# Four of the modulation sums moved from TensorE's matmuls to VectorE's multiply-adds

## The reference

```
c_act = jax.nn.silu(c)
mod = c_act @ mod_w[i] + mod_b[i]
sh_m, sc_m, gt_m, sh_f, sc_f, gt_f = [m[:, None, :] for m in jnp.split(mod, 6, axis=-1)]
h = rmsnorm(x, norm_pre_mix[i]) * (1.0 + sc_m) + sh_m
y = conformer_conv_module(h, ...)       # h @ w1, gate, depthwise convolution of width 31, layernorm, @ w2
x = x + gt_m * rmsnorm(y, norm_post_mix[i])
h = rmsnorm(x, norm_pre_ffn[i]) * (1.0 + sc_f) + sh_f
y = conv_ffn(h, ...)
```

## Time and profile before

| What | Value |
|---|---|
| Median of 3 runs | 1467.34 us (1464.78 to 1468.24) |
| The profiled execution | 1466.46 us |
| Its span in the trace | 1464.7 us |
| Granted clock over the span | 0.996 |
| TensorE / VectorE / ScalarE / GpSimd busy | 97% / 65% / 47% / 11% |
| The stretch of the convolution steps | about 55 to 129 us |

### The profile page before, as it was taken

One profiled execution on the slowest core, in us unless ns is written; L12 is line 12 of the kernel. 1 busy time (PEld: TensorE's weight loads), 2 busy tenths in 40 slices (PEclk: granted clock), 3 DMA queues, 4 the chain that ended last, 5 costly groups with the idle time before them and its releaser, 6 DMA issues.

```text
span 1464.7 us, 31335 instructions
## 1 busy us (share of the span) xinstructions
PE 1419.9 (97%) x12736; PEld 1293.8 (88%) x12737; DVE 951.1 (65%) x1289; ACT 683.9 (47%) x879; POOL 155.5 (11%) x178
## 2 busy tenths in 40 slices
PE   6999999999999999999999999999999999999997
PEld 4767789999999998988889999999999898899996
DVE  3657676667655556695677556575566678855656
ACT  4445654545534336744435343353434466534332
POOL 1343032231000004012300000000000012000000
PEclk9999999999999999999999999999999999999999
DMA  9984466666666655421026666666666344576662
GB/s 345 329 314 183 148 201 187 194 178 179 182 192 182 185 157 166 144 87 57 9 87 200 183 191 186 187 187 187 186 186 195 121 145 148 164 216 191 186 186 86
DMA packets 293909, 257.75 MB, mean 176 GB/s; under 512 B 7104, under 2 KB 270272, under 8 KB 290752
## 3 DMA queue, kind: packets, MB, share of 16 engines
q1 hardware_dynamic: 293824, 256.49, 57.3%
HBM read 255.42 MB, written 1.05 MB: 175 GB/s over the span
## 4 chain that ended last, share of the span: by engine, by line
PE 50%; DVE 4%; ACT 1%; issue 0%; DVEq 0%; ACTq 0%
PE ps L145 14%; PE ps L146 14%; PE ps L147 14%; PE ps L2306 3%; PE ps L383 1%; DVE stats L342 1%; DVE arena L340 1%; PE ps L390 1%; PE ps L469 0%; PE ps L474 0%; PE ps L470 0%; PE ps L2289 0%; PE ps L2297 0%; DVE gate_m L2609 0%; PE ps L2792 0%
## 5 line engine op out<-in xcount | busy, mean ns | idle before, releaser
L145 PE MATMUL ps<-actT,a_parts 128*128 128x256 f32 x2096 | 589.1, 281 | 8.0 <-DVE a_parts L130 4.2
L146 PE MATMUL ps<-actT,a_parts 128*128 128x256 f32 x2096 | 585.8, 279 | 0.0
L147 PE MATMUL ps<-actT,a_parts 128*128 128x256 f32 x2096 | 585.4, 279 | 0.0
L145 PEld LDWEIGHTS ps<-actT,a_parts 128*128 128x128 f32 x2096 | 394.8, 188 | 17.7 <-DVE a_parts L130 6.7
L146 PEld LDWEIGHTS ps<-actT,a_parts 128*128 128x128 f32 x2096 | 394.6, 188 | 4.2
L147 PEld LDWEIGHTS ps<-actT,a_parts 128*128 128x128 f32 x2096 | 394.6, 188 | 0.0
L1329 DVE TENSOR_TENSOR a_parts<-a_raw,a_parts 128x2048 fp32r<-128x2048 f32 x100 | 239.1, 2391 | 55.8 <-ACT a_parts L1326 55.6
L1343 DVE TENSOR_TENSOR b_parts<-b_raw,b_parts 128x1024 fp32r<-128x1024 f32 x72 | 88.2, 1225 | 160.3 <-ACT b_parts L1340 160.3
L1326 ACT ACTIVATE a_parts<-a_raw 128x2048 fp32r<-128x2048 f32 x100 | 190.3, 1903 | 0.7 <-DMA a_raw<-in_ffn_w_up 0.7
L1340 ACT ACTIVATE b_parts<-b_raw 128x1024 fp32r<-128x1024 f32 x90 | 95.2, 1058 | 171.0 <-PE ps L147 171.0
L145 PE MATMUL ps<-b_parts,hid 128*128 128x512 f32 x400 | 158.1, 395 | 1.2 <-DVE hid L1440 1.2
(11 more groups left out here) (387 smaller groups left out, 1820.1 us busy)
## 6 DMA issues: line engine op xcount, KB each, us to landing
a_raw<-in_ffn_w_gate SPq DMA_DIRECT2D x88, 512.0 KB, 4.0
a_raw<-in_ffn_w_up SPq DMA_DIRECT2D x88, 512.0 KB, 5.2
b_raw<-in_ffn_w_down SPq DMA_DIRECT2D x88, 512.0 KB, 3.3
arena<-in_mod_w SPq DMA_DIRECT2D x24, 1024.0 KB, 9.5
a_raw<-in_f_up_w SPq DMA_DIRECT2D x44, 512.0 KB, 5.0
b_raw<-in_f_down_w SPq DMA_DIRECT2D x22, 512.0 KB, 3.3
a_raw<-in_rwkv_w_in SPq DMA_DIRECT2D x10, 1024.0 KB, 5.4
a_raw<-in_sb_w_in SPq DMA_DIRECT2D x10, 1024.0 KB, 5.2
```

The source lines that it names most:

```text
L145: pe.matmul(out, lhs[0], rhs[0], start=start, stop=False)
L146: pe.matmul(out, lhs[0], rhs[1], start=False, stop=False)
L147: return pe.matmul(out, lhs[1], rhs[0], start=False, stop=stop)
```

## The change

In steps j = 0 to 3 the second chunk of the unit (9, 11, 13 and 15) is no longer summed by TensorE. VectorE does it with 8 instructions of 128 x 256: it multiplies depth part 0 by silu(c), one value per partition, and then adds part after part, each step waiting for the one before. What is left has a part of the sum on all 128 partitions, so `mod_post` uses a weight `ones` (128 x 128, all 1) for these chunks instead of `sel`. ScalarE's copy of the four chunks goes as well. Buffers of these chunks are free again by a new semaphore `mod_added`, and GpSimd sets `ones` once at the start.

```diff
+            ON_DVE = [9, 11, 13, 15]
             def load_mod(sp, i):
                 if i >= MOD_SLOTS:
-                    sp.wait_ge(mod_used, i - MOD_SLOTS + 1)
+                    if i - MOD_SLOTS in ON_DVE:
+                        sp.wait_ge(mod_added, on_dve(i - MOD_SLOTS))
+                    else:
+                        sp.wait_ge(mod_used, on_pe(i - MOD_SLOTS))
...
+            def mod_add(dve, i):
+
+                dve.wait_ge(mod_loaded[i % MOD_SLOTS], 16 * (i // MOD_SLOTS + 1))
+                dve.wait_ge(mod_posted, (i - 2) // 2 + 1 if i < 18 else i - 9)
+                total = modp[:, i % 2]
+                for k in range(KD):
+                    rows_k = mods[:, i % MOD_SLOTS, k * MOD_COLS:(k + 1) * MOD_COLS]
+                    if k == 0:
+                        ins = dve.tensor_scalar(total, rows_k, csilu[:, 0:1], None, ALU.mult)
+                    else:
+                        ins = dve.scalar_tensor_tensor(total, rows_k, csilu[:, k:k + 1], total, ALU.mult, ALU.add)
+                    if k < KD - 1:
+                        dve_steps.step(dve, ins)
+                ins.then_inc(mod_added, 1)
...
             def mod_post(pe, u):
 
-                pe.wait_ge(mod_taken, unit_chunks(u)[-1] + 1)
+                last = unit_chunks(u)[-1]
+                pe.wait_ge(mod_taken, on_pe(last))
+                if last in ON_DVE:
+                    pe.wait_ge(mod_added, on_dve(last))
...
-                                            modp[:, i % 2, h * P:(h + 1) * P], sel[:, 0:1], start=True, stop=True)
+                                            modp[:, i % 2, h * P:(h + 1) * P],
+                                            (ones if i in ON_DVE else sel)[:, 0:1], start=True, stop=True)
...
+                    pool_steps.step(pool, pool.memset(ones, 1.0))
...
                         for i in unit_chunks(UNIT_AT[j]):
-                            mod_take(act, i)
+                            if i not in ON_DVE:
+                                mod_take(act, i)
...
                         for i in unit_chunks(UNIT_AT[j]):
-                            mod_sum(pe, i)
+                            if i not in ON_DVE:
+                                mod_sum(pe, i)
...
                     for j in range(KD):
+                        if j < 4:
+                            mod_add(dve, unit_chunks(UNIT_AT[j])[-1])
                         for g in SPLIT_AT.get(j, ()):
                             ring_a.split_lo(dve, g)
```

More of the change, by code:

```diff
@@ L552, in first_block @@
         def first_block():
-            mods, u_pad, taps_w, shifted, conv, sq, sig, rstd, modp, stat32, sel, mask32, ones_mean = carve(
+            mods, u_pad, taps_w, shifted, conv, sq, sig, rstd, modp, stat32, sel, mask32, ones_mean, ones = carve(
                 (MOD_SLOTS, ACH), (2, PAD + SEQ + 2), (2, QUAD * TAPS), (2 * 4, SHIFT_LEN), (KD, SEQ), (KD, SEQ),
-                (2, SEQ), (SEQ,), (2, MOD_COLS), (KD, QUAD), (P,), (QUAD,), (P,))
+                (2, SEQ), (SEQ,), (2, MOD_COLS), (KD, QUAD), (P,), (QUAD,), (P,), (P,))
             hT = sq
@@ L576, in first_block @@
                                                                          "post_read"))
+            mod_added = sem("mod_added")
             cond_ready, cond_sig = sem("cond_ready"), sem("cond_sig")
@@ L598, in mod_bank, with on_dve, on_pe @@
                 return 2 + i % 2 if i < 8 else (3, 7)[i % 2] if i < 16 else 3 if i < 20 else 4 + i % 2
+            ON_DVE = [9, 11, 13, 15]
+            def on_dve(i):
+                return sum(1 for v in ON_DVE if v <= i)
+            def on_pe(i):
+                return i + 1 - on_dve(i)
             def post_bank(u):
@@ L611, in mod_sum @@
                 if i >= 2:
-                    pe.wait_ge(mod_taken, i if 17 <= i < 20 else i - 1)
+                    pe.wait_ge(mod_taken, on_pe(i - 1) - (i < 9))
                 if 8 <= i < 16 and i % 2:
@@ L620, in mod_take @@
             def mod_take(act, i):
-                act.wait_ge(mod_used, i + 1)
+                act.wait_ge(mod_used, on_pe(i))
                 if i >= 2:
@@ L625, in mod_take @@
                 act.activation(modp[:, i % 2], ps[:, mod_bank(i), 0:MOD_COLS], ACT.Copy).then_inc(mod_taken, 1)
+            def mod_add(dve, i):
[11 more added lines that the diff above has]
+                ins.then_inc(mod_added, 1)
             def mod_copy(dve, i):
-                dve.wait_ge(mod_used, i + 1)
+                dve.wait_ge(mod_used, on_pe(i))
                 dve.wait_ge(mod_posted, i - 9)
@@ L646, in mod_post @@
                             ps[:, 6 + c // 2, (c % 2) * MOD_COLS:(c % 2 + 1) * MOD_COLS]
-                        ins = pe.matmul(out_, sel, modp[:, i % 2], start=True, stop=True)
+                        ins = pe.matmul(out_, ones if i in ON_DVE else sel, modp[:, i % 2], start=True, stop=True)
                 ins.then_inc(mod_posted, 1)
```

## The result

The changed kernel took 1479.43 us (median of 6, 1478.42 to 1480.49) against 1466.66 us for the kernel before on the same chip (median of 6): 12.8 us more, ratio 1.0084 with a 95% interval of 1.0073 to 1.0094. The time forecast was 1476.6, the range 1469.5 to 1479.5. The median lies 0.07 us inside the upper end, and three of the six runs (1479.73, 1480.12 and 1480.49) lie above it. The profiled execution is one of these, 1480.12 us; its trace spans 1478.2 us, 13.5 more than before.

What follows compares the result with a forecast made beforehand. TensorE, busy 97% of the span, was taken to bound the kernel. 4.8 - 0.875 - 0.875 + 3.6 = +6.7 us, with the clock's +3.4 +10.1, on 1466.46 gave 1476.6 us; range 1469.5 to 1479.5.

Steps and rivals of the forecast that it cites:

- longer steps on VectorE: Rival: VectorE's sum steps take more than 0.52 us each, giving 1477.6 or 1479.4 us; chance 0.10.
- What bounds the kernel: TensorE, busy 97% of the span: whatever it wins or loses in steps 0 to 3 arrives at the end.
- The length of a sum: One chunk's sum on VectorE: seven steps of 0.52 us and a first of 0.39, 4.0 us, between 3.4 and 4.5.
- The blocking by GpSimd: GpSimd's taps halt VectorE's sum in steps 0 and 3, 1.8 us each; rival without blocking, chance 0.14.
- Steps 0 to 3: TensorE 4.8 us late in step 0, 0.875 gained in each of steps 1 and 2, 3.6 late in step 3.
- The stalls: TensorE stands waiting for VectorE's sum, about 5.7 us in step 0 and 5.1 us in step 3.
- The margin of step 1: VectorE's sum of chunk 11 is done at 75.2, 1.3 us before TensorE's convolution ends at 76.5.
- The transfers: Chunk 13's issue waits until 65.4 for VectorE's sum of chunk 9; the delay is covered and costs nothing.
- The clock: TensorE's clock halves after each of two stalls, 3.4 us in all; rival of one fall or none, with blocking, 0.27.
- the stretch at 741: Around 741 us TensorE stood 1.3 us and its clock fell from 2.4 to 1.2 GHz, priced at 1.7 us.

Runs made afterwards that it cites:

- e3_taps: e1_wait with GpSimd's taps of steps 2 and 5 held back until VectorE's sums of chunks 9 and 15 are done; 1474.46 us, +7.4 against before.
- e4_mid: e1_wait with only chunks 11 and 13 on VectorE, 9 and 15 staying on TensorE; 1471.51 us, +4.4 against before.
- e11_busy13: e8_busy with 13 unused matmuls instead of 10 filling TensorE's stall in step 3; 1473.05 us, +6.8 against before.
- e1_wait: Changed kernel with TensorE's wait before the sums of chunks 20 to 23 set back to the copy of the same bank's last chunk; 1478.16 us, +11.1 against before.
- e5_first: e1_wait with only chunk 9 on VectorE, 11, 13 and 15 staying on TensorE; 1471.64 us, +4.6 against before.
- e2_busy: e1_wait with unused matmuls on constants filling TensorE's stalls, 8 in step 0 and 7 in step 3; 1475.20 us, +8.1 against before.
- e8_busy: e2_busy with 11 and 10 unused matmuls instead of 8 and 7; 1474.67 us, +7.7 against before.
- e10_sum13: e1_wait, chunks 9, 11, 15 on VectorE, postings of steps 0 to 3 behind weight matmuls, TensorE's sum of chunk 13 behind convolve(2); 1463.08 us, -3.2 against before.

## Why the prediction was right, and where it was off

- **The number.** The mechanism was right, and the size 2.7 us short: +10.1 forecast, +12.8 measured. That the time still lies in the range, by 0.07 us, is luck. The upper end stood for longer steps on VectorE, which did not come; a dearer clock and a wait that the forecast missed took their place.
- **What bounds the kernel.** Right: the lateness of 11.59 us at step 4 was still 11.58 at the sum of chunk 20.
- **The length of a sum.** 4.0 us forecast, 4.08 measured; line 649 at 0.485, the first instruction 0.34 to 0.44, and 0.04 us between steps. By the Trainium skill (VectorE: DVE Perf Modes, "The DRAIN you can't avoid") a flush of 0.22 us would lie between two steps (an estimate from that page). These rows do not show it.
- **The blocking by GpSimd.** Right in kind, shown by e3_taps; 1.8 us forecast, 1.53 measured. The taps themselves took 2.09 us instead of 1.92.
- **Steps 0 to 3.** +4.8, -0.875, -0.875, +3.6 forecast; +4.42, -0.81, -0.87, +3.46 measured. The pair of sums in step 3 gave back 1.34 us (2.34 before, 91.60 to 92.60 changed), not 1.46. The stalls were 5.25 and 4.73 us, where the forecast had 5.7 and 5.1. The sum of chunk 11 was 4.0 us early (74.68 against 78.73), not 1.3, since the clock had slowed TensorE, and that of chunk 13 1.6 us. The margin of step 1 exists only behind the stall of step 0. I had written the time with that stall in it, but took it in e4_mid's expectation for a property of the step; e4_mid showed a stall of 4.03 us there.
- **The transfers.** Right: no wait in steps 1 and 2, though SP issued chunk 13 late.
- **The clock.** This term was mis-sized: 3.4 us forecast, 5.4 in the trace. The times of e11_busy13 against e1_wait say 4.3, too widely to tell the two apart. I had priced a fall at 1.7 us, from the stretch at 741, where the clock was back after 3.4 us. Here it stayed down for 5.3 us of work behind step 0 and 6.3 behind step 3, which cost 2.48 and 2.91 us.
- **What was missed.** One step of the forecast was wrong, the reading of the changed wait counts. It looked at the four chunks that move and took the wait of every other sum as unchanged. The sums of chunks 20 to 23 waited longer, which cost 2.4 us in the trace and 1.7 in the times of e1_wait. With both corrections the sum is 6.2 + 5.4 + 2.4 = 14.0 for a span that grew by 13.5.

## What to carry to other kernels

Work that is taken off the busiest engine and given to one with a low mean load is only free if the second engine has room between its last duty and the moment the result is asked for; that is to be counted at each place, and counted again without the stalls that an earlier place causes. If there is no room, first move the point at which the result is asked for: four sums on VectorE cost 12.8 us, and three of them gained 3.2 once the posting and the sum of chunk 13 stood elsewhere and the stricter wait was set back. And where wait counts are rewritten, every wait on that semaphore has to be gone through, not only those of the moved work.

## What the runs showed of the hardware

- What a fall of the clock costs varies. Behind the stall of step 0 TensorE worked at 1.2 GHz for 4.7 us in e1_wait, 5.3 in the changed kernel and 7.7 in e5_first, which cost 2.2, 2.5 and 3.5 us. Behind step 3 of e2_busy and e8_busy a fall cost 1.6.
- The clock can fall when TensorE is already at work again. In e2_busy TensorE worked from 100.33 us on, and the granted clock was 1.00 until 102 and 0.64 from 102 to 103.
- How long TensorE stood does not by itself say whether the clock falls. It stayed up behind 1.6 us idle in step 0 of e2_busy, fell behind 1.08 us in step 3 of e8_busy, fell in e10_sum13 behind 1.76 us at 48 us, where the other profiles with 1.2 to 1.6 us there show none, and fell in e1_wait behind the 2.3 us idle at 21 us, where it stayed up in the kernel before. What tells these apart is open.
- A multiply-add on VectorE with both inputs in SBUF stood still while GpSimd ran its two-input taps: 2.01 us instead of 0.485. When the taps were held back (e3_taps) the longest was 0.488.
